# The in-chunk attention levels on 32-column TensorE tiles: a change to a fused HGRN2, gMLP and cross-attention layer

## What is computed

```python
b = jnp.cumsum(logf, axis=1)
causal = jnp.tril(jnp.ones((C, C), dtype=bool))
diff = b[:, :, None] - b[:, None, :]
decay = jnp.exp(jnp.where(causal[None, :, :, None, None], diff, -jnp.inf))
A = jnp.einsum('bthk,bshk,btshk->bhts', q, k, decay)
o = (jnp.einsum('bhts,bshv->bthv', A, v)
     + jnp.einsum('bthk,bhkv->bthv', q * jnp.exp(b), S))
k_dec = k * jnp.exp(b_last[:, None] - b)
S_new = jnp.exp(b_last)[..., None] * S + jnp.einsum('bshk,bshv->bhkv', k_dec, v)
```

## Time and profile before

| | |
|---|---|
| median of 3 runs | 3116.57 us (3115.3 to 3117.15) |
| the profiled execution: its own time | 3125.33 us |
| its span | 3123.5 us |
| PE busy | 3004.9 us, 96%, 14642 matmul records |
| weight loads (PEld) busy | 2448.8 us, 78% |
| DVE busy | 1335.1 us, 43% |
| ACT busy | 776.6 us, 25% |
| POOL busy | 478.6 us, 15%, nearly all in the first block |

### The profile page before, as it was taken

The page is one execution under the profiler, slowest core; times in us unless marked ns, Lnnn a source line. Parts: engine busy times, 40 slices in busy tenths (PEclk is TensorE's granted clock), DMA queues, the critical chain, the costliest instruction groups (busy, mean ns, idle before and its releaser), DMA issues.

```text
span 3123.5 us, 35547 instructions
## 1 busy us (share of the span) xinstructions
PE 3004.9 (96%) x14642; PEld 2448.8 (78%) x14642; DVE 1335.1 (43%) x2364; ACT 776.6 (25%) x984; POOL 478.6 (15%) x389
## 2 busy tenths in 40 slices
PE   7889899999999999999999999999999999999997
PEld 6768788677778888778888878877778887877786
DVE  5568723443244743322234572322324483332222
ACT  4424412110023522201024441210103452110011
POOL 0185412788750000000000000000000000000000
PEclk9898999999999999999999999999999999999999
DMA  7694365997966345575666435566767525566754
GB/s 264 258 342 161 124 220 194 346 351 246 320 240 246 109 148 177 193 260 200 217 226 223 145 115 189 190 228 244 275 230 283 173 97 175 181 232 245 259 191 137
DMA packets 207515, 675.57 MB, mean 216 GB/s; under 512 B 22721, under 2 KB 28097, under 8 KB 207361
## 3 DMA queue, kind: packets, MB, share of 16 engines
q1 hardware_dynamic: 199760, 660.58, 60.3%
q10 hardware_dynamic: 7600, 12.78, 1.1%
HBM read 542.80 MB, written 130.48 MB: 216 GB/s over the span
## 4 chain that ended last, share of the span: by engine, by line
PE 85%; DVE 8%; ACT 3%; DMA 2%; issue 1%; SPq 1%; POOL 0%; DVEq 0%; ACTq 0%; POOLq 0%
PE half L861 74%; PE half L987 3%; PE half L869 2%; PE half L1137 2%; DVE lvl L1992 1%; DVE lvl L2010 1%; PE half L876 1%; DMA w_raw<-in_w_up 1%; DVE bb L2064 1%; DVE uu L2132 1%; PE half L1042 1%; PE half L982 0%; DMA w_pairs<-stage 0%; PE half L1147 0%; DVE xn L1657 0%
## 5 line engine op out<-in xcount | busy, mean ns | idle before, releaser
L861 PE MATMUL half<-a_hi,w_ring 128*128 128x512 f32 x2560 | 827.6, 399 | 7.0 <-POOL w_ring L801 6.9
L861 PE MATMUL half<-w_ring,a_hi 128*128 128x512 f32 x2176 | 683.4, 396 | 0.0
L861 PE MATMUL half<-w_ring,ht_hi 128*128 128x512 f32 x2048 | 637.5, 393 | 0.0
L861 PEld LDWEIGHTS half<-a_hi,w_ring 128*128 128x128 f32 x2560 | 483.2, 189 | 140.3 <-issue 23.1
L861 PE MATMUL half<-a_lo,w_ring 128*128 128x512 f32 x1280 | 507.7, 397 | 0.0
L861 PEld LDWEIGHTS half<-w_ring,a_hi 128*128 128x128 f32 x2176 | 415.1, 191 | 92.2
L861 PE MATMUL half<-w_ring,a_lo 128*128 128x512 f32 x1088 | 438.0, 403 | 21.6 <-ACT vv L1524 12.3
L861 PEld LDWEIGHTS half<-w_ring,ht_hi 128*128 128x128 f32 x2048 | 385.4, 188 | 83.8
L861 PE MATMUL half<-w_ring,ht_lo 128*128 128x512 f32 x1024 | 401.7, 392 | 0.7 <-DVE qq_s L1819 0.7
L2215 DVE SCALAR_TENSOR_TENSOR x<-half,rstd,x 128x512 f32<-128x512 f32 x256 | 174.5, 744 | 303.0 <-PE half L861 303.0
L861 PEld LDWEIGHTS half<-a_lo,w_ring 128*128 128x128 f32 x1280 | 241.9, 189 | 56.5
(11 more groups left out here) (295 smaller groups left out, 2777.5 us busy)
## 6 DMA issues: line engine op xcount, KB each, us to landing
w_ring<-w_pairs SPq DMA_DIRECT2D x704, 512.0 KB, 3.3
w_pairs<-w_ring SPq DMA_DIRECT2D x192, 512.0 KB, 4.9
w_pairs<-stage SPq DMA_DIRECT2D x16, 1024.0 KB, 4.6
w_raw<-in_w_up SPq DMA_DIRECT2D x64, 256.0 KB, 4.5
w_raw<-in_w_down SPq DMA_DIRECT2D x64, 256.0 KB, 4.0
w_s<-in_w_up SPq DMA_DIRECT2D x8, 2048.0 KB, 11.2
w_s<-in_w_down SPq DMA_DIRECT2D x8, 2048.0 KB, 11.8
w_raw<-in_w_in SPq DMA_DIRECT2D x48, 256.0 KB, 3.8
```

Source lines behind the costliest of these rows:

```text
L861: m = nc.tensor.matmul(ps[:, j, :], l, r, start=(i == 0 and q == 0), stop=(i == tiles_in - 1 and q == 2))
```

## The change

- Each level is cut into column tiles of 32 keys. For levels 0 to 5 each of the four groups of 32 tokens only meets itself: weights 128 x 32, moving columns 32 (level 0) or 16, output on the group's own 32 partitions, all six levels in one bank (bank 3 of the unit's half) in 64 columns each. Level 6 has two such products of 32 columns per head, level 7 two of 64, into bank 2. That makes 28 matmuls per head, 56 per unit, where there were 16.
- The levels are no job of their own any more: they go to banks 2 and 3 of the half whose banks 0 and 1 the unit's ("out", u) uses.
- Keys and queries are one tensor `kq`, and cumulated logarithms one tensor `bn` with their negatives beside them (one operation of 2048 elements per block makes these). A subtraction reads minus or plus b for left and right halves (`signed`), so exponents have the sign that Exp wants, ACT takes no absolute values, and `scaled` makes one product per level of 256 elements instead of two of 128. `ends` has one product of 512 elements instead of a copy, a subtraction and two products; `e_last` comes from ACT.
- `attention` works on 192, 256, 64, 64 and 256 elements instead of 1024, 512, 256 and 256.
- DVE's order per unit is now `attention(u)`, `new_state(u - 1)`, `args(u + 2)`, `scaled(u + 1)`, then the rest; before, it was `args(u + 2)`, `attention(u)`, the rest, `scaled(u + 2)`, `new_state(u)`. `rows_and_state(u)` waits for `att_ready` of u and for `ends_ready` of u + 1, a new event that stands ahead of the level products of `scaled`.
- The gMLP product is 4 operations of 512 elements instead of 16 of 128. SP waits for `att_ready` of the last unit before it loads x. At the start DVE rearranges the masks in 7 small operations.

```diff
@@ -115,7 +117,7 @@
...
-    jobs += [(h, ("lv", u))] + {6: [(1, "zu")], 7: [(1, "otu")]}.get(u, []) + [(h, ("out", u))]
+    jobs += {6: [(1, "zu")], 7: [(1, "otu")]}.get(u, []) + [(h, ("out", u))]
...
@@ -478,6 +483,22 @@
...
+def unit(t, u):
+    c, p = divmod(u, 2)
+    return t[..., c, 2 * p:2 * p + 2, :]
+def signed(t, u, w, i=None):
+    one = unit(t[:, 0], u)
+    n, step = (w // 2, 1) if i is None else (w // 2, 0)
+    return bass.AP(one.tensor, one.offset + (i or 0),
+                   [one.ap[0], [w, 2 * P // w], [TT * H * P + (w // 2 if i is None else 0), 2], [step, n]])
+def by_head(t):
+    return t.rearrange("p c h t -> p h c t")
...
@@ -659,7 +680,7 @@
...
-    sp.wait_ge(*out(pos, ("lv", UNITS - 1)))
+    sp.wait_ge(att_ready.sem, att_ready.at(pos, UNITS - 1))
...
@@ -968,29 +989,36 @@
...
+    if u == SWAP:
+        pe.wait_ge(*out(pos, "zg"))
+    ps = out_of(pos, ("out", u))
+    for j in range(2):
+        keys, queries = kq[:, 0, c, 2 * p + j], kq[:, 1, c, 2 * p + j]
+        for l in range(LEVELS):
+            w = 1 << l
+            if l:
+                keys = queries = lvl[u % 2][:, l - 1, j, :]
+            for g in range(P // GROUP):
+                own = slice(g * GROUP, g * GROUP + GROUP)
+                if l < GROUP_LEVELS:
+                    to = ps[own, 3, (2 * l + j) * GROUP:(2 * l + j + 1) * GROUP]
+                    q = queries[:, own]
+                    if l:
+                        to, q = (t.rearrange("p (n w) -> p n w", w=w)[:, :, w // 2:] for t in (to, q))
+                else:
+                    if g * GROUP % w >= w // 2:
+                        continue
+                    right = slice(g * GROUP // w * w + w // 2, g * GROUP // w * w + w)
+                    to, q = ps[own, 2, j * P + right.start:j * P + right.stop], queries[:, right]
+                m = nc.tensor.matmul(to, keys[:, own], q, start=True, stop=True)
+    m.then_inc(levels_done.sem, 1)
...
+        m = nc.tensor.transpose(ps[:, 1, (2 + j) * P:(3 + j) * P], ends[u % 3][:, 0, j, :], ident[:])
...
@@ -1001,14 +1029,15 @@
     if u >= 2:
         pe.wait_ge(added_used.sem, added_used.at(pos, u - 2))
     if u + 1 < UNITS:
-        pe.wait_ge(scaled_ready.sem, scaled_ready.at(pos, u + 1))
+        pe.wait_ge(ends_ready.sem, ends_ready.at(pos, u + 1))
+    pe.wait_ge(att_ready.sem, att_ready.at(pos, u))
     ps = begin(pos, ("out", u))
     for j in range(2):
         h = 2 * p + j
         v = vv[:, c, h * P:h * P + P]
         o = ps[:, 0, j * P:j * P + P]
         nc.tensor.matmul(o, att[:, j, :], v, start=True, stop=False)
-        nc.tensor.matmul(o, ends[u % 3][:, 0, j, :], state[:, h, :], start=False, stop=True)
+        nc.tensor.matmul(o, ends[u % 3][:, 1, j, :], state[:, h, :], start=False, stop=True)
         m = nc.tensor.matmul(ps[:, 1, j * P:j * P + P], kdt[:, j, :], v, start=True, stop=True)
     if u + 1 < UNITS:
         m = keys_to_rows(ps, u + 1)
@@ -1476,12 +1505,12 @@
...
-nc.scalar.activation(ends[u % 3][:], ends[u % 3][:], ACT.Abs)
-nc.scalar.activation(lvl[u % 2][:], lvl[u % 2][:], ACT.Abs).then_inc(act_sem, 1)
-act.wait_ge(act_sem, link.next())
-nc.scalar.activation(ends[u % 3][:], ends[u % 3][:], ACT.Exp, scale=-1.0)
-nc.scalar.activation(lvl[u % 2][:], lvl[u % 2][:], ACT.Exp, scale=-1.0
-                     ).then_inc(decays_ready.sem, 1)
+minus, b = unit(bn[:, 0], u), unit(bn[:, 1], u)
+for j in range(2):
+    nc.scalar.activation(ends[u % 3][:, 0, j, :], minus[:, j, :], ACT.Exp, bias=b[:, j, P - 1:P])
+nc.scalar.activation(ends[u % 3][:, 1], b, ACT.Exp)
+nc.scalar.activation(e_last[u % 3][:], b[:, :, P - 1], ACT.Exp)
+nc.scalar.activation(lvl[u % 2][:], lvl[u % 2][:], ACT.Exp).then_inc(decays_ready.sem, 1)
...
@@ -1509,13 +1538,14 @@
...
-nc.scalar.activation(kk[:], out_of(pos, "zf")[:], ACT.Sigmoid, scale=-1.0)
-nc.scalar.activation(bb[:], out_of(pos, "zf")[:], ACT.Sigmoid).then_inc(evacuated_of(pos, "zf"), 1)
+zf = out_of(pos, "zf")[:].rearrange("p h (c t) -> p h c t", c=TT)
+nc.scalar.activation(by_head(kq[:, 0]), zf, ACT.Sigmoid, scale=-1.0)
+nc.scalar.activation(by_head(bn[:, 1]), zf, ACT.Sigmoid).then_inc(evacuated_of(pos, "zf"), 1)
...
-    ins = nc.scalar.activation(bb[:, h, :], bb[:, h, :], ACT.Ln, scale=oml[:, h:h + 1],
+    ins = nc.scalar.activation(bn[:, 1, :, h, :], bn[:, 1, :, h, :], ACT.Ln, scale=oml[:, h:h + 1],
...
@@ -1728,6 +1759,11 @@
...
+for g in range(1, P // GROUP):
+    rows = slice(g * GROUP, g * GROUP + GROUP)
+    for i in (slice(0, 3), slice(4, 7, 2)):
+        nc.vector.tensor_copy(masks[rows, i, 0:GROUP], masks[rows, i, rows])
+nc.vector.tensor_tensor(masks[:, 3], masks[:, 7], masks[:, 5], ALU.subtract)
...
@@ -1977,64 +2013,54 @@
...
+    ins = nc.vector.tensor_tensor(lvl[u % 2][:, l - 1].rearrange("p j (n a w) -> p (j n) a w", a=2,
+                                                                 w=w // 2),
+                                  signed(bn, u, w), signed(bn, u, w, w // 2 - 1), ALU.subtract)
+ins.then_inc(args_ready.sem, 1)
...
+nc.vector.tensor_tensor(ends[u % 3][:], ends[u % 3][:], unit(kq, u), ALU.mult
+                        ).then_inc(ends_ready.sem, 1)
...
+    v = lvl[u % 2][:, l - 1].rearrange("p j (n a w) -> p (j n) a w", a=2, w=w // 2)
+    ins = nc.vector.tensor_tensor(v, v, signed(kq, u, w), ALU.mult)
...
+ps = out_of(pos, ("out", u))
+wide = ps[:, 2, 0:2 * P].rearrange("p (j t) -> p j t", j=2)
+v = ps[:, 3, 0:GROUP_LEVELS * 2 * GROUP].rearrange("p (a e j t) -> p a e j t", a=3, e=2, j=2)
+def own_size(i, n=1):
+    return masks[:, i:i + n, None, 0:GROUP].bitcast(mybir.dt.int32).to_broadcast([P, n, 2, GROUP])
+nc.vector.tensor_copy(yt[:, 36:37], ident[:, 0:1])
+nc.vector.copy_predicated(v[:, :, 0], own_size(0, 3), v[:, :, 1]).then_inc(dve_sem, 1)
+nc.vector.copy_predicated(att[:], masks[:, 5:6, :].bitcast(mybir.dt.int32).to_broadcast([P, 2, P]), wide)
...
+nc.vector.copy_predicated(v[:, 0:1, 0], own_size(4), v[:, 1:2, 0]).then_inc(dve_sem, 1)
...
+nc.vector.copy_predicated(v[:, 0:1, 0], own_size(6), v[:, 2:3, 0]).then_inc(dve_sem, 1)
...
+nc.vector.tensor_copy(yt[:, 36:37], ident[:, 0:1])
+groups = [P, 2, P // GROUP, GROUP]
+nc.vector.copy_predicated(att[:].rearrange("p j (g t) -> p j g t", t=GROUP),
+                          masks[:, 3:4, :].bitcast(mybir.dt.int32).rearrange(
+                              "p j (g t) -> p j g t", t=GROUP).to_broadcast(groups),
+                          v[:, 0, 0, :, None, :].to_broadcast(groups)).then_inc(att_ready.sem, 1)
...
@@ -2056,28 +2082,34 @@
...
-    nc.vector.tensor_scalar(kk[:, h, :], kk[:, h, :], oml[:, h:h + 1], None, ALU.mult)
+    nc.vector.tensor_scalar(kq[:, 0, :, h, :], kq[:, 0, :, h, :], oml[:, h:h + 1], None, ALU.mult)
...
-        s = bb[:, h, c * P:c * P + P]
+        s = bn[:, 1, c, h, :]
...
+dve.wait_ge(dve_sem, link.next())
+nc.vector.tensor_scalar(bn[:, 0], bn[:, 1], -1.0, None, ALU.mult).then_inc(dve_sem, 1)
...
+nc.vector.memset(att[:], 0.0)
...
-nc.vector.tensor_tensor(qq[:], qq[:], out_of(pos, "zq")[:], ALU.mult
-                        ).then_inc(evacuated_of(pos, "zq"), 1)
+nc.vector.tensor_tensor(by_head(kq[:, 1]), by_head(kq[:, 1]), out_of(pos, "zq")[:].rearrange(
+    "p h (c t) -> p h c t", c=TT), ALU.mult).then_inc(evacuated_of(pos, "zq"), 1)
...
-scaled(1)
...
-    dve.wait_ge(*done(pos, ("lv", u)))
+    dve.wait_ge(levels_done.sem, levels_done.at(pos, u))
+    attention(u)
+    if u:
+        new_state(u - 1)
...
-    attention(u)
+    if u + 1 < UNITS:
+        scaled(u + 1)
...
@@ -2110,15 +2142,12 @@
...
-    if u + 2 < UNITS:
-        scaled(u + 2)
...
-    new_state(u)
...
@@ -2126,13 +2155,13 @@
...
-        for t in range(TT):
-            for g in range(H):
-                c = slice(g * P, g * P + P)
-                ins = nc.vector.scalar_tensor_tensor(uu[:, t, c], ps[:, t, c], bs_col[:, g:g + 1],
-                                                     uu[:, t, c], ALU.add, ALU.mult)
+        for g in range(H):
+            c = slice(g * P, g * P + P)
+            ins = nc.vector.scalar_tensor_tensor(uu[:, :, c], ps[:, :, c], bs_col[:, g:g + 1],
+                                                 uu[:, :, c], ALU.add, ALU.mult)
...
+new_state(UNITS - 1)
...
```

68 lines of the change are left out of this document (12 added, 56 removed).

## The result

The changed kernel takes 3047.95 us (median of four runs, 3046.19 to 3051.18), against 3116.6; the ratio is 0.9781, interval 0.9765 to 0.9798. The forecast was 3047. The profiled execution took 3046.88 us, with a span of 3044.9.

The account below looks back on a forecast made before the run. The prediction took PE, busy for 96% of the span, as the bound. Three later blocks at 17.5 us (52.5) plus 17 for the first made 69.5, so 3116.57 became 3047; the 8-in-10 range was 3024 to 3098.

Parts of the forecast that it names:

- The level products: Each unit's level stage on PE: column groups overlap, 1.5 us instead of 3.69, saving 2.2 us per unit.
- The rival with a least distance of 20 to 31 ns: Level stage: issue spaces records by 20 to 31 ns whatever their group; 3071 to 3107 us, middle 3088; chance 0.21.
- The rivals without overlap and with a falling clock: Level stage: groups wait for each other, 3107 us or more, chance 0.05; small tiles lower PE's clock, about 3169, chance 0.08.
- `uu`: gMLP product on DVE at each block's end: four operations take 2.6 us instead of 4.24, 1.6 less per block.
- DVE's chain in the later blocks: DVE's work behind each unit's levels takes 7.9 us, PE wants it after 9.9, so it is hidden.
- The rival with DVE as the bound: Per unit, DVE's loop takes 3 us more than summed and PE waits; 3082 us; chance 0.06.
- the stall and its slow clock stay, at nothing: Unit 4 of later blocks: the 3.0 us gate wait and 9.3 us at 1.2 GHz stay, so no gain there.
- The first block: First block: 7 x 2.2 + 1.6 as in a later block, 17 us saved.
- The bounds (5 and 30): First block's saving: 5 us if DVE's loop takes all level savings, 30 if five waits each shorten by 2 to 3.
- the operation that makes the negatives (L2093), put at nothing: DVE, once per block behind the projections: 2.4 us, hidden, so nothing, or 2.4 per block if that cover is gone.
- Unit 0's 0.5: PE's idle 0.55 us before unit 0's levels, a wait for ACT, goes: 0.5 less per later block.
- The sum: Whole kernel: 52.5 us from three later blocks plus 17 from the first, 69.5 off the median 3116.57.

Follow-up runs that it names:

- one_group: The changed kernel with all 112 level records of a unit sent to column group 0 (attention matrices come out wrong): 3123.86 us, ratio 1.0013.
- group_major: The changed kernel with, for each head, all level products of one column group before the next group's, not in turn: 3099.66 us, ratio 0.9928.
- uu16: The changed kernel with the gMLP product back in 16 operations of 128 elements: 3058.18 us, ratio 0.9808.
- args_first: The changed kernel with DVE's new_state(u - 1) and args(u + 2) ahead of attention(u): 3037.44 us, ratio 0.9739.

## Why the prediction was right, and where it was not

- **The level products.** Forecast 1.5 us per stage and 2.2 saved per unit; measured 1.26 and 2.1 to 2.3 (mean of six plain units 13.1 / 6 = 2.18). The stage is 0.24 shorter than the forecast, and yet no more was saved: the 3.69 us that it was set against is unit 1's, where units 2, 3, 5 and 6 took 3.49 before (unit 2: 1044.88 to 1048.37), and 0.1 is lost behind it. That the two misses cancel is luck. The reasoning that the groups overlap is shown by one_group and group_major: the same records in one group cost 33 ns each, close to the 31 of the earlier trace rows, and the change's gain is gone.
- **The rival with a least distance of 20 to 31 ns** fell: four groups in turn start 10 ns apart. The Trainium skill's floor of about 25 ns between starts ("TensorE: Matmul & The Clock Gate", section "Wait — 56ns, not 53.3ns?") is not what this trace shows for products that go to different column groups; within one group the least here is 31 to 32, above the floor. The rivals without overlap and with a falling clock fell with the same rows: 10 ns in turn, and a PEclk of 1.00 in the units behind (windows above).
- **`uu`**: forecast 2.6 us, measured 2.73; 1.5 less per block instead of 1.6, and uu16 shows it on the path.
- **DVE's chain in the later blocks**: forecast 7.9 us behind the levels, measured 7.9. The rival with DVE as the bound holds only in the first block.
- **Unit 4.** The step "the stall and its slow clock stay, at nothing" was wrong in its second half. The stall stayed, 3.6 us where it was 3.0; the wait of 0.5 us for `att` that stood ahead of it is now part of it. The slow clock did not: in the second block the window's excess over a plain unit fell from 4.5 (17.90 - 13.40) to 1.7 us (12.96 - 11.27). In the second block of the kernel before, all of unit 4's levels were made at 1.2 GHz (PEclk 0.50) and took 6.8 us (1072.80 to 1079.61) instead of 3.49. In the second block of the changed kernel they are over before the clock falls (1040.38 to 1041.63, 1.25 us at PEclk 1.00). The step took the low-clock stretch for a fixed price, when the slow stage lay inside it. Unit 4 in the changed kernel's third and last block, then a plain unit and unit 4 of one_group:

```profile
1753.49:1765.77 12.28, 11.45 (x163) 9.51 (x163) 9.89 (x27) 5.34 (x13) 0.00 (x0) 1.00 0.32 97
2459.24:2473.10 13.86, 13.86 (x162) 11.56 (x162) 9.89 (x27) 5.35 (x13) 0.00 (x0) 0.78 0.29 87
```

```profile
1029.71:1043.60 13.89, 13.89 (x164) 12.12 (x163) 9.85 (x30) 5.92 (x14) 0.00 (x0) 1.00 0.35 116
1072.30:1090.55 18.25, 18.25 (x162) 15.95 (x162) 9.88 (x27) 5.35 (x13) 0.00 (x0) 0.72 0.19 64
```

  With the same stall of 3.6 us the clock is low for a part of unit 4 in the second block and the last, and not at all in the third. The excess in the three later blocks is 1.7, 1.0 (0.83 of it the stop shown above) and 2.6 us with a stage of 1.26; 2.9, 3.7 and 3.8 with 2.95 (group_major); 4.4, 3.9 and 3.7 with 3.86 (one_group); 4.5, 3.3 and 4.9 in the kernel before with 3.49. So the short stage stands apart from the others, and among these the excess doesn't go by the stage's length. Why the clock is low for less time with the short stage no run isolates. In the three blocks together unit 4 gained some 7.5 us beyond the levels' saving, where the forecast had nothing.
- **The first block**: forecast 17, measured 21, 13.1 in its units and 8 ahead of them; up to 5.8 of these 21 may be of the one profile of before, as said above. The bounds (5 and 30) held it, the working did not. The units gained less than the 17.0 counted: PE's busy time fell by 21.5 us (112.18 to 90.73), but its idle time rose by 8.3 (13.1 to 21.4), by the new waits for `ends` and `lvl` (10.3 us, where 9.1 of waits for `att` stood), for `uu` (2.7, was 0.9) and for the gate (3.6, was 1.5) and by smaller ones. Ahead of the units 8 us came, of which the sum had none: the working named ACT's absolute values of `lvl`, 1.6 us, and did not add them. What it missed: ACT's exponentials are 5.05 us earlier (225.81 against 230.86), since the absolute values of `ends` and `lvl` and two rounds of operations on `ends` are gone ahead of them, and behind them the 8.68 us of products at L2010 are no longer the last to be ready, `gemm` is. Against that stands the operation that makes the negatives (L2093), put at nothing: it takes 2.14 us on that chain, from 204.15 on. Which of these gives how much was not tried apart.
- **Unit 0's 0.5** (the wait for `kdt`) came, and was given back: the rest of each block is 0.75 to 1.0 us longer. Windows of the first 3.4 us behind the block's end, in the changed kernel and in the one before:

```profile
1086.67:1090.00 3.33, 3.33 (x9) 2.67 (x10) 2.16 (x10) 0.60 (x3) 0.00 (x0) 0.55 0.69 273
```

```profile
1129.88:1133.30 3.42, 3.42 (x15) 2.82 (x16) 2.17 (x10) 1.55 (x3) 0.00 (x0) 1.00 0.97 389
```

  Behind the chain of `uu`, PE works at 1.2 GHz there (PEclk 0.55), where it ran at 2.4 before. The idle time of the block's end now is more in one piece, 2.9 us ahead of the output projection where it was 1.6. That this is what lets the clock fall was not tried.
- **The sum.** The trace gained 78.6 us and the forecast summed 69.5; the medians gained 68.7. That the predicted median came within 1 us is in part chance: the sum was some 9 us low against the trace, and the profiled execution of before was 8.7 us slower than its median. The second was written down beside the sum; the first was not seen, and up to 5.8 of its 9 us are part of the second.
- **What the forecast did not ask**: whether each part of the change helps. It put the new order of DVE down as hidden, and args_first is 10 us faster without it. Some of that is the path: the order delays `args`, `args` delays ACT's exponentials, and these stand ahead of the gate activation that frees unit 4's half. The prediction said that ACT begins it at a fixed time after unit 3's levels, and did not add up ACT's queue in the new order. The time came out the same by chance, 9.0 us after the levels' end in both kernels (1061.75 to 1070.78, 1029.40 to 1038.36): `args` is done 1.7 us later, and ACT needs 1.8 us less without the absolute values. So the new order spent what ACT's shorter work had won.

## What to carry to other kernels

When many small products are bound by their weights' columns, cut them so that neighbours in the queue go to different column groups: here 112 records cost 1.26 us in turn, 2.95 group by group, 3.86 in one group. Read the queues of the engines off the bound for what they free (PSUM halves) and not for how busy they are; a queue's first blocked instruction sets the time of all behind it, and moving ACT's gate activation and the copies behind it ahead of its exponentials was worth 13 us, where one_group, with 73 us less work on DVE, was no faster than the kernel before. A stall is removed only when what comes next in the same place is ready too, so look one wait further before you cost it.

## What the runs showed of the hardware that was not expected

- Starts of matmul records 10 ns apart over a whole stage, with four column groups in turn, where the starts within one group are 31 to 32 ns apart.
- PE stopping for 0.3 to 3.8 us with nothing to wait for, when 168 or 224 records with their weight loads follow each other at that pace: in 9 and in 23 of 32 stages. The cause is open.
- Behind one and the same stall of 3.6 us TensorE's clock fell to 1.2 GHz in two of three later blocks of one execution and stayed at 2.4 GHz in the third (mean PEclk of unit 4: 0.87, 1.00, 0.78). Unit 4 lost 1.0 to 2.6 us with a level stage of 1.26 us, and 2.9 to 4.9 with stages of 2.95 to 3.86.
